# Partial sums, a head norm by blocks of tokens, and a new order in the delta rule

## The reference, cut to what matters

```python
# before every projection: the norm of the residual stream x (width 1024)
y = xf * lax.rsqrt(jnp.mean(xf * xf, axis=-1, keepdims=True) + EPS)
# after the differential attention: the same over each head's 128 outputs (4 heads, 512 and 256 tokens)
o = rms_norm(o, subln_g) * (1.0 - lambda_init)
# the gated delta rule: 4 heads, forwards and backwards, in chunks of tokens
tmat = triangular_solve(eye + lower, eye)           # per chunk, from k alone
def step(s, xs):                                    # from chunk to chunk
    v_new = u_c - w_c @ s
    o = qd_c @ s + a_c @ v_new
    return s * jnp.exp(gl_c) + jnp.swapaxes(kd_c, -1, -2) @ v_new, o
```

## Time and profile before

| | us |
|---|---|
| median of three runs (range) | 3793.63 (3790.63 to 3793.81) |
| profiled execution | 3794.6 |
| its span | 3792.8 |
| PE busy in the span | 3520.9 (93%) |
| DVE busy | 1945.5 (51%) |
| ACT busy | 822.4 (22%) |
| POOL busy | 1432.8 (38%) |

### The profile page before, as it was taken

One profiled execution on the slowest core, in us unless ns is written; L12 is line 12 of the kernel. 1 busy time (PEld: TensorE's weight loads), 2 busy tenths in 40 slices (PEclk: granted clock), 3 DMA queues, 4 the chain that ended last, 5 costly groups with the idle time before them and its releaser, 6 DMA issues. The chain is left out here.

```text
span 3792.8 us, 50133 instructions
## 1 busy us (share of the span) xinstructions
PE 3520.9 (93%) x20654; PEld 2806.6 (74%) x20654; DVE 1945.5 (51%) x3179; ACT 822.4 (22%) x1614; POOL 1432.8 (38%) x653
## 2 busy tenths in 40 slices
PE   6897978999998989868999799899999899899998
PEld 3684567888886878757888566788888577788887
DVE  5797653223436656683233457953243368752342
ACT  3212512110002233301100235522000244521001
POOL 2322034224564322205455322345445323354454
PEclk9998989999999999989999899999999899999999
DMA  5443412221113200112332222223332222223332
GB/s 178 138 154 117 176 45 62 67 62 61 57 50 84 70 16 2 65 36 73 95 100 95 57 80 56 68 73 100 95 95 83 65 78 56 74 78 100 95 95 78
DMA packets 399792, 305.91 MB, mean 81 GB/s; under 512 B 11292, under 2 KB 367462, under 8 KB 398983
## 3 DMA queue, kind: packets, MB, share of 16 engines
q1 hardware_dynamic: 397464, 302.19, 26.2%
q10 hardware_dynamic: 2095, 0.44, 0.1%
HBM read 296.30 MB, written 6.29 MB: 80 GB/s over the span
## 5 line engine op out<-in xcount | busy, mean ns | idle before, releaser
L450 POOL TENSOR_TENSOR low<-raw,high 128x1024 fp32r<-128x1024 f32 (+1 forms) x437 | 1054.8, 2414 | 1746.9 <-DVE high L356 1746.9
L519 PE MATMUL scores<-high 128*128 128x512 f32 (+1 forms) x1944 | 737.6, 379 | 74.4 <-DVE low L704 31.3
L519 PE MATMUL scores<-low,high 128*128 128x512 f32 (+1 forms) x1944 | 723.9, 372 | 0.0
L519 PE MATMUL scores<-high,low 128*128 128x512 f32 (+1 forms) x1944 | 722.3, 372 | 0.0
L356 DVE CAST high<-raw 128x1024 fp32r<-128x1024 f32 (+1 forms) x437 | 396.4, 908 | 506.6 <-PE scores L519 263.9
L519 PE MATMUL bank<-high 128*128 128x512 f32 (+1 forms) x1480 | 542.0, 366 | 0.0
L519 PE MATMUL bank<-low,high 128*128 128x512 f32 (+1 forms) x1480 | 538.9, 364 | 0.0
L519 PE MATMUL bank<-high,low 128*128 128x512 f32 (+1 forms) x1480 | 538.3, 364 | 0.0
L519 PEld LDWEIGHTS scores<-high 128*128 128x128 f32 x1944 | 372.5, 192 | 158.1 <-POOL low L450 54.8
L519 PEld LDWEIGHTS scores<-high,low 128*128 128x128 f32 x1944 | 372.5, 192 | 64.4
L519 PEld LDWEIGHTS scores<-low,high 128*128 128x128 f32 x1944 | 373.4, 192 | 60.7 <-issue 1.0
(11 more groups left out here) (639 smaller groups left out, 4931.8 us busy)
## 6 DMA issues: line engine op xcount, KB each, us to landing
raw<-in_mlp_w SPq DMA_DIRECT2D x128, 512.0 KB, 4.0
raw<-in_w_in SPq DMA_DIRECT2D x76, 512.0 KB, 3.9
ring<-in_ada_w SPq DMA_DIRECT2D x32, 1024.0 KB, 7.1
raw<-in_w_gate SPq DMA_DIRECT2D x44, 512.0 KB, 3.8
raw<-in_w_up SPq DMA_DIRECT2D x44, 512.0 KB, 3.7
raw<-in_w_down SPq DMA_DIRECT2D x40, 512.0 KB, 3.4
mix<-in_ada_w SPq DMA_DIRECT2D x16, 1024.0 KB, 6.5
raw<-in_od_w_in SPq DMA_DIRECT2D x29, 512.0 KB, 3.8
```

The lines of the kernel that those rows point to most:

```text
L450: pool.tensor_tensor(tile(low, u), tile(raw, u), tile(high, u).bitcast(F32), ALU.subtract)\
L519: mm = pe.matmul(out(p), stationary, moving, start=(k0 + k == 0 and i == 0), stop=(k0 + k == job.kc - 1 and i == len(pairs) - 1))
```

## The change

1. `SquareSums`, where x is at most 512 wide (`narrow`): six half tiles instead of three tiles; GpSimd adds only chunks 1 to 3, TensorE sums tile 0 and chunks 4 to 7; only the squares of chunks 3 and 7 wait for a tile. The small Sqrt waits for the third addition.
2. `head_norm`: sums are kept by blocks of 128 tokens in groups of 32 rows, in one bank for the 512 tokens and one for the 256; there are two roots and two reciprocals of 128 columns, and the spreading works by blocks of 128 columns.
3. `delta_rule`: a new order. PE reads the state before it turns the blocks and sums the gates before the first level; the state's products stand behind a level's seconds and ahead of the next firsts; the Gram products stand behind `query_grams`. DVE stores and computes the first direction's right-hand side ahead of part 0; the second direction's comes in two halves behind levels 1 and 2; exponents come together behind level 3; `advance` is split.

The places at which the order is not plain from the text are shown whole:

```diff
...
         self.m, self.x, self.toks, self.width = m, x, toks, toks[-1][0] + toks[-1][1]
+        self.narrow = self.width <= 512
+        self.n_added = 3 if self.narrow else DC - 3
...
     def tile(self, c):
+        if self.narrow:
+            half = (0, 2, 1, 2, 3, 4, 5, 1)[c]
+            return self.ring[:, half // 2, 512 * (half % 2):512 * (half % 2) + self.width]
         return self.ring[:, 0 if c == 0 else 1 + c % 2, 0:self.width]
+    def tile_free(self, act, c):
+        if self.narrow:
+            if c in (3, DC - 1):
+                act.wait_ge(self.added, 1 if c == 3 else 2)
+        elif c >= 3:
+            act.wait_ge(self.added, min(c - 2, DC - 3))
...
             if self.at[c] == u:
-                if c >= 3:
-                    act.wait_ge(self.added, min(c - 2, DC - 3))
+                self.tile_free(act, c)
                 self.stored(act, self.job, c, self.parts - 1)
...
         if u == self.end:
-            act.activation(self.ring[:, 0, 1023:1024], self.m.eps[:, 0:1], ACT.Sqrt).then_inc(self.begun, 1)
+            if self.narrow:
+                act.wait_ge(self.added, 3)
+            unused = self.ring[:, 1, 0:1] if self.narrow else self.ring[:, 0, 1023:1024]
+            act.activation(unused, self.m.eps[:, 0:1], ACT.Sqrt).then_inc(self.begun, 1)
     def gpsimd(self, pool, u):
-        for c in range(1, DC - 2):
+        for c in range(1, self.n_added + 1):
             if self.at[c] == u:
...
                 self.stored(pe, self.job, self.first, s)
-            pe.wait_ge(self.added, DC - 3)
-            for c in (0, DC - 2, DC - 1):
+            pe.wait_ge(self.added, self.n_added)
+            for c in (0, *range(self.n_added + 1, DC)):
                 if c:
...
     n = len(units)
-    with buffers(nc, sq=[P, 3, T], roots=[P, T]) as (sq, roots), \
+    SUMS = 0, 5
+    with buffers(nc, sq=[P, 3, T], roots=[P, 2 * P]) as (sq, roots), \
             stage(nc, "squared", "summed", "rooted", "inverted", "spread", "scaled", "gated") as \
...
                 act.activation(sq[:, i % 3, 0:tn], o[:, c, t0:t0 + tn], ACT.Square).then_inc(squared, 1)
-            act.wait_ge(summed, n)
-            act.activation(roots[:, :], m.bank[0][:, :], ACT.Sqrt, **inverse_root(P)).then_inc(rooted, 1)
+            for s, (t0, tn) in enumerate(toks):
+                rows = 32 * (tn // P)
+                act.wait_ge(summed, chunks * (s + 1))
+                act.activation(roots[0:rows, s * P:(s + 1) * P], m.bank[SUMS[s]][0:rows, 0:P], ACT.Sqrt, **inverse_root(rows))\
+                    .then_inc(rooted, 1)
...
                 pe.wait_ge(squared, i + 1)
-                pe.matmul(m.bank[0][:, 0:tn], m.row_picker(i, P), sq[:, i % 3, 0:tn],
-                          start=(i == 0), stop=(i == n - 1)).then_inc(summed, 1)
-            pe.wait_ge(inverted, 1)
+                for j in range(tn // P):
+                    mm = pe.matmul(m.bank[SUMS[s]][32 * j:32 * j + 32, 0:P], m.row_picker(c, 32), sq[:, i % 3, j * P:(j + 1) * P],
+                                   start=(c == 0), stop=(c == chunks - 1))
+                mm.then_inc(summed, 1)
             for i, (c, s) in enumerate(units):
                 tn = toks[s][1]
+                pe.wait_ge(inverted, s + 1)
                 if i >= 4:
                     pe.wait_ge(scaled, i - 3)
-                pe.matmul(m.bank[1 + i % 4][:, 0:tn], m.ident[:, i:i + 1].broadcast_to([P, P]),
-                          roots[:, 0:tn], start=True, stop=True).then_inc(spread, 1)
+                rows = 32 * (tn // P)
+                for j in range(tn // P):
+                    mm = pe.matmul(m.bank[1 + i % 4][:, j * P:(j + 1) * P],
+                                   m.ident[0:rows, 32 * j + c:32 * j + c + 1].broadcast_to([rows, P]),
+                                   roots[0:rows, s * P:(s + 1) * P], start=True, stop=True)
+                mm.then_inc(spread, 1)
...
         def _(dve):
-            dve.wait_ge(rooted, 1)
-            dve.reciprocal(roots[:, :], roots[:, :]).then_inc(inverted, 1)
+            for s, (t0, tn) in enumerate(toks):
+                r = roots[0:32 * (tn // P), s * P:(s + 1) * P]
+                dve.wait_ge(rooted, s + 1)
+                dve.reciprocal(r, r).then_inc(inverted, 1)
             for i, (c, s) in enumerate(units):
...
-            def level(k, lv):
+            def firsts(k, lv):
+                for s in both:
+                    first(s, k, lv)
+            def seconds(k, lv):
                 for s in both:
...
                         second(s, k, lv)
-                if lv == 5 and k + 1 < n_chunks:
-                    for s in both:
-                        grams(s, k + 1)
-                if lv < 6:
-                    for s in both:
-                        first(s, k, lv + 1)
...
                 j, more, has = k - 1, k < n_chunks, k > 0
-                if more:
-                    for s in both:
-                        turn_blocks(s, k)
                 if has:
...
                     for s in both:
-                        first(s, k, 1)
+                        turn_blocks(s, k)
                 if k + 1 < n_chunks:
...
                 if more:
-                    level(k, 1)
+                    firsts(k, 1)
+                    seconds(k, 1)
                 if has:
...
                 if more:
-                    level(k, 2)
+                    firsts(k, 2)
+                    seconds(k, 2)
+                if has:
+                    update(both[0], j)
+                if more:
+                    firsts(k, 3)
+                    seconds(k, 3)
                 if has:
                     new_values(both[1], j)
-                    update(both[0], j)
                 if more:
-                    level(k, 3)
+                    firsts(k, 4)
+                    seconds(k, 4)
                 if has:
...
                 if more:
-                    level(k, 4)
+                    firsts(k, 5)
+                    seconds(k, 5)
                 if has:
                     query_grams(both[1], j)
+                if k + 1 < n_chunks:
+                    for s in both:
+                        grams(s, k + 1)
                 if more:
-                    level(k, 5)
+                    firsts(k, 6)
                 if has:
...
                 if more:
-                    level(k, 6)
+                    seconds(k, 6)
                 if has:
...
-            def right_hand_side(s, k):
-                dve.wait_ge(s.starts_raised, k + 1)
-                step(dve.scalar_tensor_tensor(out=s.ecol[:, :], in0=s.ecol[:, :], scalar=-1.0,
-                                              in1=beta[:, s.order[k], s.heads], op0=ALU.mult, op1=ALU.mult))
-                dve.wait_ge(s.read, k + 1)
-                dve.wait_ge(s.values_scaled, k + 1)
-                for h in range(HEADS):
+            def right_hand_side(s, k, heads=range(HEADS)):
+                if heads[0] == 0:
+                    dve.wait_ge(s.starts_raised, k + 1)
+                    step(dve.scalar_tensor_tensor(out=s.ecol[:, :], in0=s.ecol[:, :], scalar=-1.0,
+                                                  in1=beta[:, s.order[k], s.heads], op0=ALU.mult, op1=ALU.mult))
+                    dve.wait_ge(s.read, k + 1)
+                    dve.wait_ge(s.values_scaled, k + 1)
+                for h in heads:
                     ins = dve.scalar_tensor_tensor(out=s.rhs[:, H(h)], in0=s.value_bank[:, H(h)],
...
                                                    op0=ALU.mult, op1=ALU.add)
-                ins.then_inc(s.rhs_ready, 1)
+                if heads[-1] == HEADS - 1:
+                    ins.then_inc(s.rhs_ready, 1)
...
                 j, more, has = k - 1, k < n_chunks, k > 0
+                if j > 0:
+                    for s in both:
+                        store(s, j - 1)
+                if has:
+                    right_hand_side(both[0], j)
                 if more:
...
                         begin_turned(s, k)
-                if j > 0:
-                    for s in both:
-                        store(s, j - 1)
-                if more:
                     for s in both:
...
                         part(s, k, 1)
+                    subtract_both(k, 1)
                 if has:
-                    right_hand_side(both[0], j)
+                    right_hand_side(both[1], j, range(0, 2))
                 if more:
-                    subtract_both(k, 1)
                     for s in both:
                         part(s, k, 2)
+                    subtract_both(k, 2)
                 if has:
-                    right_hand_side(both[1], j)
+                    right_hand_side(both[1], j, range(2, HEADS))
                 if more:
-                    subtract_both(k, 2)
                     for s in both:
                         part(s, k, 3)
+                    subtract_both(k, 3)
                 if k + 1 < n_chunks:
-                    end_exponents(both[0], k + 1)
```

(14 more changed lines are left out.)

## The result

The kernel after took 3764.25 us (median of four runs, 3759.10 to 3767.12), the one before 3793.72 beside it: a ratio of 0.9922, 95% interval 0.9906 to 0.9938, or 29.5 us less by medians. The profiled execution took 3759.1 (span 3757.3), the fastest of the four, so a stage-by-stage comparison must leave about 5 us unexplained. Where two profiles are compared by stage, the same two instructions bound the stretch in both, and the text names them.

A forecast was written before the change was run, and what follows sets the result against it. PE, busy in 93% of the span, was taken as the bound, gains coming where it waits or isn't the bound. Delta rule 18.2, `SquareSums` 3.6 and head norm 6.2 made 28.0 us: 3766, own range 3761 to 3771.

The forecast's parts named there:

- Head norm: Head norm: squares run through, smaller root and reciprocal, spreading 0.8 dearer; 6.2 us saved, bounds 1.8 to 7.0.
- SquareSums: Ends of the two second layers: last square follows x at once, 1.8 us each; 3.6 saved, bounds 2.4 to 4.4.
- Levels: Delta rule, levels 1 to 4: 2.1 us saved in each of chunks 1 to 3, 2.6 and 4.5 in 4 and 5; 13.4.
- A filled level: Delta rule: a level with one state product, now between seconds and firsts, takes 3.3 us instead of 3.91.
- Chunk starts: Delta rule: 2.9 us saved in chunks 1 and 2 each, 1.5 in 3; 0.9 and 1.6 lost in 4 and 5; 4.8.
- Rival (a): Delta rule: DVE becomes the bound, XT slow wherever GpSimd runs; only 9 us saved there, 3775 in all; chance 0.20.
- a sign of being wrong: Delta rule: forecast wrong if PE's largest wait is for `part` or the right-hand side.
- The sign on the clock: Delta rule: forecast wrong if PE's granted clock there isn't above 0.95.
- the waits for XT: Delta rule: PE's waits for XT fall from 10.6 us to under 3.
- Rival (d): Delta rule: PE meets `new_values` or `update` before DVE's input is ready, each miss costing 3.3 us; slower, 3812; chance 0.03.
- Rival (c): Head norm: PE slow throughout, only 1.8 us saved there, the rest as forecast; 3770; chance 0.07.
- The 2.5 times: Head norm: by the skill's short-matmul rule spreading by blocks takes 2.5 times as long, head norm loses 1; 3773; chance 0.03.

The follow-up runs named there:

- the other run: Kernel after, with GpSimd waiting for both directions' first XT from chunk 1 on and ten unread PE products in the head norm: 3762.68 us, 0.9917 of the kernel before.
- Factors together: Kernel after, with GpSimd waiting from chunk 3 on, both right-hand-side factors made at chunk start, five unread PE products in the head norm: 3758.65 us.

## Why the prediction was right, point by point

- **Total.** 3766.0 forecast, 3764.25 and 3765.39 measured. Head norm, `SquareSums` and delta rule: forecast 6.2, 3.6, 18.2; by stages 6.3, 3.5, 19.8 (19.3 with what stands ahead of the first turned block). The delta rule is as close as it is partly by luck: levels and starts gave 3.0 more than forecast, and a term of 1.7 that I had overlooked took part of it back.
- **Levels.** A filled level 3.3, measured 3.38. Levels 1 to 4: 1.9 and 1.5 saved in chunks 1 and 2 (forecast 2.1 each), 2.5 in chunk 3, 3.0 (2.6) and 5.4 (4.5) in chunks 4 and 5: 14.3 against 13.4. The difference is one step that I counted in the wrong place. I had both sets of query Grams on top of levels 1 to 4, and none in chunk 3; after, one set stands behind level 5. From there to the outputs' end chunks 3 to 5 are 0.8 longer each, chunks 1 and 2 are 0.4 shorter, in all 1.7 that the saving must give back.
- **Chunk starts.** Forecast 4.8; measured from the last seconds' end to level 1's seconds 3.1, 3.1, 2.3, -0.4, -1.1, together 6.9. Chunks 1 and 2 as worked out (6.2 against 6.3). In chunk 3 the start took 6.8, I had 7.7; the run without new starts shows that it takes 7.7 in the old order too when the clock does not fall. Why it fell behind the wait of 1.57 us in the kernel before and not in that run, no run shows. So of what chunk 3 gained at its start most was PE's clock, not the order, and that chunk as a whole gained nothing by it (31.8 against 32.2). In chunks 4 and 5 the losses were 0.4 and 1.1, not 0.9 and 1.6. Chunk 0, put at 0, gave 0.3 up to its last seconds; 14.3 + 6.9 - 1.7 + 0.3 are the 19.8.
- **Rival (a)** did not come as a bound but was there in small: XT at 1.04 to 1.19 us beside GpSimd, `ecol` at 0.79, `part` the largest wait of TensorE (2.7 us). The prediction had set that as a sign of being wrong; it was too sharp, since the same row stands with a stage that gained more than forecast. The sign on the clock (not above 0.95) could not tell either, as the stage had 0.96 before the change. And the waits for XT fell to 1.2 by the line of the earlier trace rows but to 3.0 with the first XT of a chunk, not under 3. I had priced the overlap at XT alone and overlooked `ecol`, because it has 4 columns and takes 0.12 us by itself.
- **Rival (d)** asked whether a hand-over could be missed. None was in the kernel after. The runs of one order alone show that it is no idle fear: with DVE's order missing, the gates of chunk 4 stood 3.2 us in front of the queue; with PE's missing, the right-hand side did.
- **`SquareSums`.** The place is shown (1.76 per execution by profile), the time is not shown by the run of it alone: 0.7 by medians with an interval from 8 us gained to 0.8 lost.
- **Head norm.** Squares 3.77 against 3.6, reciprocals 1.75 for two, as the earlier trace rows had it for one (0.95), end 14.45 us behind the first square against 14.6. The spreading was slow for its first 4.6 us; what I took from the earlier trace rows held. **Rival (c)** did not come: from 498.3 on the granted clock was 1.00. The 2.5 times that the prediction worked out from the Trainium skill, page "TensorE: Matmul & The Clock Gate", section "Back-to-back issue gap", did not come either: at full clock eight instructions of 128 columns took 0.99 us to the start of the next group, against 0.86 for two of 512 in the kernel before, 1.15 times.

## What to carry to other kernels

When two engines play ping-pong, work that isn't part of the game belongs into each one's own idle, and both orders must be changed together: here either alone gave 6 us or cost 5, both gave 19. Before an engine's product is moved ahead of another, list what it waits for on the other engine and where that stands in the queue there. And price a two-input DVE instruction beside GpSimd by what GpSimd has left to do, not by its own size. Do that in every round of the loop: the last version cured chunks 3 to 5 and lost a microsecond in the round behind them.

## What the runs showed of the hardware

- **A DVE instruction with both inputs in SBUF waits for GpSimd's.** XT (128x256) took 0.42 alone and up to 1.19 beside GpSimd; `ecol` (128x4) 0.12 and 0.92. Instructions with one input in PSUM kept their time beside it (`part` 0.41, `rhs` 0.3 each). GpSimd pays too: its two decays of the state took 2.2 to 2.4 beside XT and 2.03 without. The Trainium skill, page "SBUF — State Buffer", section "SBUF: two separate sides", describes an exclusive lock for the whole instruction; the 0.92 of a four-column instruction agrees.
- **PE can be kept at its upper level by products nobody reads.** Five products of 128 columns in an idle of 2.3 us: spreading 2.94 instead of 4.57 for 24 instructions, at a granted clock of 1.00 instead of 0.63. In the other run ten products began at 0.50, and it was 1.00 from 491.5 on.
- **How long PE stays at the lower level behind nearly the same idle differs.** The gates of chunk 0, same code in both kernels, behind two waits of 2.25 us together (1.98 and 0.27, 1.65 and 0.60). The kernel after, where the granted clock is 0.50 from 1385.5 to 1388.0 and 1.00 from 1388.8:

```profile
1387.22 1.75 PE L2463 MATMUL scores<-tri,g 128*128 128x128 f32 x8
1388.80 1.06 PE L2463 MATMUL bank<-tri,g 128*128 128x128 f32 x8
```

Factors together, where it is still 1.00 at 1388.2 and 0.50 from 1388.7 to 1394.5:

```profile
1389.85 2.07 PE L2465 MATMUL scores<-tri,g 128*128 128x128 f32 x8
1391.71 1.92 PE L2465 MATMUL bank<-tri,g 128*128 128x128 f32 x8
```

That makes chunk 0 take 23.5 or 25.2 us. Two profiles of the kernel after had the short form, both variants of it the long one. The delta rule alone, whose code there is that of the kernel after, had 2.04 and 1.85 for the two rows, so the variants' additions are not needed for it. What decides was not settled.
